# Interleaving the first two input units of a two-layer hybrid trunk, with the head of the kernel reordered

## Chip, core and metric

The kernel runs on one core of one Trainium2 chip. The metric is the device time of one execution in microseconds (us). Time before: 1334.67 us, the median of three runs (1334.59 to 1341.18).

## The reference, cut to what matters

Input x is 512 positions by 1024 features, and there are two layers of this form (layer 0 and layer 1):

```python
for l in range(2):
    h = rms_norm(x, norm_mix_g[l])
    aq, ak, av, rq, rk, rv, rg, sz, sxbc, sdt = split(h @ w_in[l])
    ya = swa_sink_attention(aq, ak, av, ...)     # head group A
    yr = retention(rq, rk, rv, rg, ...)          # head group B
    ys = ssd_mixer(sz, sxbc, sdt, ...)           # head group C: conv with 4 taps, then SSD
    x = x + concat([ya, yr, ys]) @ w_out[l]
    h = rms_norm(x, norm_ffn_g[l])
    x = x + conv_ffn(h, ...)
return rms_norm(x, final_norm_g)
```

`rms_norm(x, g)` is x / sqrt(mean(x*x) + eps) * g. The mean runs over the 1024 features.

## The kernel before, in words

Features lie on partitions: x is 8 tiles (o = 0 to 7) of 128 features by 512 positions. All dense products are split into high and low parts: a weight w is w_hi + w_lo and an activation h is h_hi + h_lo, each part in the type fp32r, and a product is three matmuls (h_hi by w_hi, h_lo by w_hi, h_hi by w_lo).

**Units.** A dense unit Dn makes 128 output columns. Of a layer, D0 to D27 are the input projection, each over 8 tiles of k, 24 matmuls of 128x512. The output projection and the FFN follow. Unit n accumulates in the PSUM bank dense[n % 2], so it waits until VectorE has evacuated unit n - 2 (semaphore evac). All matmuls go through the helpers at line 924. In a unit (`unit`) the high parts of a pack's tiles come first (two matmuls for each k) and then the low parts of its weights.

**Weights.** They come as a stream of packs, 4 tiles of 128x128 in 256 KB each, into 4 slots. For each pack SyncE's queue issues the fetch into w_raw, ScalarE makes w_hi by a copy (lines 405 and 418), GpSimd makes w_lo by a subtraction (line 359). `unit_tiles` and `segments` (SEGS, UNIT_END, PACK_END) lay the units into packs; `weight_stream` on the host fills the packs in the same order. ScalarE splits ahead: at step D of unit n it goes up to two packs behind the unit's last pack, or four where it has something to await there. The fetch of pack 4 in layer 0 is issued behind the eight transfers of the attention bias (lines 301 to 307).

**The norm.** The gain g is in h, and 1/sqrt of the mean (rstd) is multiplied in when a unit is evacuated. So D0 can start before rstd is known, but no unit of the input projection can be evacuated. For each tile o, ScalarE makes h_hi (line 381) and the square (386), VectorE makes h_lo (607) and adds the square to ssq (613), all in `norm_tile`. Square o waits for the addition o - 2, since there are two square buffers. In layer 0 this runs while x is being fetched (lines 291 to 295); for the later norms it runs behind the evacuations of the units before. The step NORM on TensorE (`norm`) is one matmul of ones by ssq into bank mix5. In `rms` ScalarE turns it into rstd: Ln (391) and Exp (394), each with a table load of its own. DT is the projection onto the eight dt columns, 24 matmuls into the same bank mix5; it waits until Ln has read the bank.

**The order.** SCHEDULE is a list written by hand, which every engine follows in program order. It begins `D0 NORM D1 DT D2 DTB D3 D4 DTC D5 D6 DTD D7 D8 TOK`. VectorE evacuates each D with rstd (line 664). D0, D1, D3, D4, D6 and D7 hold conv columns (U_CONV): behind each of these evacuations VectorE runs four dependent tap instructions (671 and 674), and ScalarE a silu (446). D2, D5 and D8 are evacuated only. VectorE's parts of DT, DTB, DTC and DTD (687 to 708) are a chain of small instructions on 8 partitions, with ScalarE's parts (467 to 475) between them. VectorE enters each layer by waiting for rstd; behind this wait stand two memsets (627, 628) and wdt_lo (630), and then the steps.

**The start.** TensorE first waits for `rel` and makes two small matmuls for the attention bias, and then goes to D0.

Of the kernel before, what the change touches and what calls it, by code (L numbers as in the profile page):

```python
# [19 lines left out]
D, S, P = 1024, 512, 128  # L20
# [11 lines left out]
SLOTS = 4  # L32
# [17 lines left out]


def segments():


    units, unit_end, pack_end, at, n = [], [], {}, 0, 0
    for tiles in unit_tiles():
        runs, k = [], 0
        while k < tiles:
            m = min(4 - at % 4, tiles - k)
            n += 1  # L60
            runs.append((at // 4, at % 4, k, m))
            at, k = at + m, k + m
            pack_end[(at - 1) // 4] = n
        units.append(runs)
        unit_end.append(n)
    return units, unit_end, [pack_end[i] for i in range(at // 4)], n
# [7 lines left out]
SCHEDULE = (  # L74
# [92 lines left out]
def build(nc, a, out):  # L167
    f32, f32r = mybir.dt.float32, mybir.dt.float32r
    ALU, ACT, AX = mybir.AluOpType, mybir.ActivationFunctionType, mybir.AxisListType
    with ExitStack() as ctx:  # L170
# [100 lines left out]
        f_scaled, f_conv, f_silu = sem("f_scaled"), sem("f_conv"), sem("f_silu")  # L271
        f_prod, f_hi, f_lo = sem("f_prod"), sem("f_hi"), sem("f_lo")
        relt_mm, relt_ready, rel_written = sem("relt_mm"), sem("relt_ready"), sem("rel_written")
        bias_loaded, setup_done = sem("bias_loaded"), sem("setup_done")
# [13 lines left out]
        def _(sp):  # L288
            sp.dma_start(p_all[:, :], a["params"]).then_inc(p_loaded, 16)
            sp.dma_start(ar("relh")[0:32, :], a["rel"]).then_inc(rel_loaded, 16)  # L290
            for o in range(KD):
                sp.dma_start(x[:, o, :], a["xT"][o]).then_inc(x_loaded[o], 16)
                if o % 2:
                    s = o // 2
                    sp.dma_start(w_raw[:, s, :], a["w"][s]).then_inc(raw_loaded[s], 16)
# [68 lines left out]
        def _(act):  # L364
# [10 lines left out]
            def norm_tile(e, o, l_evac):  # L375

                if l_evac is None:
                    act.wait_ge(x_loaded[o], 16)
                else:
                    act.wait_ge(evac, l_evac)  # L380
                nc.scalar.activation(h_hi[:, o, :], x[:, o, :], ACT.Copy,  # L381
                                     scale=gcol(e, o)).then_inc(h_hi_ready, 1)
                if o >= 3:
# [15 lines left out]
            act.wait_ge(p_loaded, 16)  # L399
            first_packs = {2: (0,), 5: (1,), KD - 1: (2, 3)}  # L400
            for o in range(KD):
                norm_tile(0, o, None)
                for s in first_packs.get(o, ()):
                    act.wait_ge(raw_loaded[s], 16)
                    nc.scalar.activation(w_hi[:, s, :], w_raw[:, s, :], ACT.Copy).then_inc(hi_ready, 1)  # L405
            act.wait_ge(c_loaded, 16 * N_CONST_LOADS)

# [173 lines left out]
        def _(dve):  # L581
# [10 lines left out]
            def gcol(e, o):  # L592
                return par["g"][:, bass.ds(e * KD + o, 1)]

            for i in range(6):
                V.memset(rstd[:, i:i + 1], 0.0).then_inc(m_free[i], 1)
# [7 lines left out]
            def norm_tile(e, o):  # L604

                dve.wait_ge(h_hi_ready, e * 8 + o + 1)
                V.scalar_tensor_tensor(h_lo[:, o, :], x[:, o, :], gcol(e, o), h_hi[:, o, :].bitcast(f32),  # L607
                                       ALU.mult, ALU.subtract).then_inc(h_lo_ready, 1)
                if o:
                    dve.wait_ge(sq_ready, e * 8 + o + 1)  # L610
                    if o > 1:
                        dve.wait_ge(ssq_added, e * 7 + o - 1)
                    V.tensor_tensor(ssq[:, :], ssq[:, :], sq[:, o % 2, :], ALU.add).then_inc(ssq_added, 1)  # L613

            for o in range(KD):
                norm_tile(0, o)
            dve.wait_ge(c_loaded, 16 * N_CONST_LOADS)
            with dve.Fori(0, DEPTH) as l:
                base[0] = l * DVE_LINKS
                links[0] = 2  # L620
                dve.wait_ge(rstd_ready, l * 2 + 1)

                def lo_from(dst, src, hi, done):
# [6 lines left out]
                V.tensor_tensor(wdt_lo[:, :], wdt_raw[:, bass.ds(l * 64, 64)], wdt_hi[:, :].bitcast(f32),  # L630
                                ALU.subtract).then_inc(wdt_lo_ready, 1)
                for name in SCHEDULE:
                    step, n = step_of(name)
# [286 lines left out]
        def _(pe):  # L920
            T = nc.tensor

            def mm(dst, lhsT, rhs, start=True, stop=True):
                return T.matmul(dst, lhsT, rhs, start=start, stop=stop)  # L924

            pe.wait_ge(rel_loaded, 16)

            mm(dense[0][0:8, 0:191], relw, relh).then_inc(relt_mm, 1)
            mm(dense[1][0:8, 0:8], relw, relw).then_inc(run_done, SEG0)
            pe.wait_ge(relt_ready, 1)  # L930

            def unit(bankno, number, runs, src_hi, src_lo, wait_for_tile=None):

                pe.wait_ge(evac, number + 1)
                d = dense[bankno][:, :]
                last = runs[-1][3] + runs[-1][4] - 1
# [38 lines left out]
            with pe.Fori(0, DEPTH) as l:  # L975
                def dense_unit(n, src, wait_for_tile=None):
                    runs = [(p % SLOTS, l * N_PACKS + p, t0, k0, m) for p, t0, k0, m in SEGS[n]]
                    unit(n % 2, l * N_UNITS + n, runs, *src, wait_for_tile)

                def ret_tile(k):  # L980
# [278 lines left out]
def weight_stream(w_in, w_out, w_up, w_down):  # L1259
# [14 lines left out]

    def unit(w, out_cols):
        tiles.extend(w[P * k:P * k + P][:, out_cols] for k in range(w.shape[0] // P))

    for l in range(DEPTH):
        for c in cols:
            unit(w_in[l], c)  # L1280
        for part in range(3):
# [64 lines left out]
```

## Time and profile before

| | us |
|---|---|
| median of three runs | 1334.67 |
| the runs | 1334.59, 1334.67, 1341.18 |
| the profiled execution: time | 1339.34 |
| its span | 1337.6 |
| TensorE busy | 1296.2 (97%) |
| weight load on TensorE | 1042.3 (78%) |
| VectorE busy | 634.7 (47%) |
| ScalarE busy | 627.4 (47%) |
| GpSimd busy | 577.7 (43%) |

The span is what the profile covers; the execution's own time has a little more around it. Busy shares are averages over the whole span, and stages differ. PE is TensorE, PEld its weight load, DVE VectorE, ACT ScalarE, POOL GpSimd and SP SyncE with its DMA queue. PEclk is the granted TensorE clock as a share of 2.4 GHz. At the head, until the first change that it recorded, the profile shows 1.00 whatever the pace; there the durations of the matmuls tell it.

### The profile page before, as it was taken

Reading aid. Unit: us, or ns where it says so; the run is one execution under the profiler, and the core shown is the slowest. Engines: PE = TensorE matmul, PEld = TensorE weight load, DVE = VectorE, ACT = ScalarE, POOL = GpSimd, SP = SyncE. Lnnn points to the kernel's source line nnn. Section 1 sums busy time; section 2 is a strip of 40 time slices with the busy share of each in tenths; the row PEclk is TensorE's granted clock in tenths of the full one; section 3 lists DMA queues with packets and bytes.
Section 4 is the critical chain, followed back from the end, with each engine's and each line's share of the span. In section 5 each row is a group of like instructions: output and inputs, shape, how many; then the busy total and the mean of one; then the engine's idle time right before and its main releaser. Section 6 shows DMA issues by size and latency. Waiting matters only on the chain.

```text
span 1337.6 us, 21561 instructions
## 1 busy us (share of the span) xinstructions
PE 1296.2 (97%) x6130; PEld 1042.3 (78%) x6130; DVE 634.7 (47%) x957; ACT 627.4 (47%) x961; POOL 577.7 (43%) x433
## 2 busy tenths in 40 slices
PE   6999999999999999999999999999999999999995
PEld 4777777777888888888877777777788888888884
DVE  6845567366444203443267546664744430144423
ACT  6432285356666323333363225825676652233433
POOL 2533344154444544444444334333454444444443
PEclk9999999999999999999999999999999999999998
DMA  6334222132333322332223432121323333223232
GB/s 193 111 104 111 64 79 76 35 103 79 102 94 94 110 95 84 97 99 95 98 81 104 118 87 79 58 69 55 103 88 101 100 97 101 95 94 94 94 103 102
DMA packets 77305, 125.32 MB, mean 94 GB/s; under 512 B 7672, under 2 KB 20248, under 8 KB 77112
## 3 DMA queue, kind: packets, MB, share of 16 engines
q1 hardware_dynamic: 77240, 124.47, 30.2%
q8 instruction: 38, 0.62, 0.2%
q14 instruction: 27, 0.22, 0.0%
HBM read 121.89 MB, written 2.55 MB: 93 GB/s over the span
## 4 chain that ended last, share of the span: by engine, by line
PE 81%; DVE 10%; issue 5%; ACT 2%; DVEq 1%; DMA 0%; ACTq 0%; SPq 0%
PE dense L924 74%; PE mix L924 6%; DVE arena L674 2%; DVE h_lo L607 2%; DVE ssq L613 1%; ACT w_hi L418 1%; PE mix L1095 1%; DVE arena L696 1%; DVE arena L769 0%; DVE arena L671 0%; DVE pad L664 0%; DMA x<-in_xT 0%; DVE mx L799 0%; DVE arena L805 0%; DVE arena L872 0%
## 5 line engine op out<-in xcount | busy, mean ns | idle before, releaser
L359 POOL TENSOR_TENSOR w_lo<-w_raw,w_hi 128x512 fp32r<-128x512 f32 x428 | 577.3, 1365 | 749.7 <-ACT w_hi L418 735.0
L924 PE MATMUL dense<-h_hi,w_hi 128*128 128x512 f32 x1152 | 458.1, 398 | 14.8 <-ACT w_hi L405 6.3
L924 PE MATMUL dense<-h_lo,w_hi 128*128 128x512 f32 x1152 | 450.8, 391 | 0.0
L418 ACT ACTIVATE w_hi<-w_raw 128x512 fp32r<-128x512 f32 x424 | 249.3, 622 | 186.1 <-PE dense L924 181.3
L924 PE MATMUL dense<-h_hi,w_lo 128*128 128x512 f32 x1152 | 309.8, 391 | 0.0
L924 PEld LDWEIGHTS dense<-h_hi,w_hi 128*128 128x128 f32 x1152 | 217.7, 189 | 67.7 <-issue 14.1
L924 PEld LDWEIGHTS dense<-h_lo,w_hi 128*128 128x128 f32 x1152 | 217.6, 189 | 46.7 <-issue 2.5
L924 PEld LDWEIGHTS dense<-h_hi,w_lo 128*128 128x128 f32 x1152 | 217.4, 189 | 45.7
L924 PE MATMUL dense<-m_hi,w_hi 128*128 128x512 f32 x544 | 217.3, 400 | 3.2 <-ACT w_hi L418 2.5
L924 PE MATMUL dense<-m_lo,w_hi 128*128 128x512 f32 x544 | 211.9, 390 | 0.0
L924 PE MATMUL dense<-m_hi,w_lo 128*128 128x512 f32 x544 | 146.8, 389 | 0.0
L924 PEld LDWEIGHTS dense<-m_hi,w_hi 128*128 128x128 f32 x544 | 102.1, 188 | 29.0 <-DVE x L655 3.3
L924 PEld LDWEIGHTS dense<-m_lo,w_hi 128*128 128x128 f32 x544 | 102.1, 188 | 23.0 <-issue 2.4
L924 PEld LDWEIGHTS dense<-m_hi,w_lo 128*128 128x128 f32 x544 | 102.1, 188 | 21.4
L908 DVE TENSOR_TENSOR x<-dense,x 128x512 f32<-128x512 f32 x32 | 22.1, 691 | 193.7 <-PE dense L924 193.7
L889 DVE SCALAR_TENSOR_TENSOR arena<-arena,params 128x512 f32<-128x512 f32 x44 | 53.1, 1206 | 62.7 <-ACT arena L559 62.7
L886 DVE TENSOR_TENSOR arena<-dense,rstd 128x512 f32<-128x512 f32 x44 | 30.5, 692 | 107.1 <-PE dense L924 107.1
L566 ACT ACTIVATE m_hi<-arena 128x512 f32 x44 | 27.8, 632 | 92.5 <-DVE arena L899 92.5
L381 ACT ACTIVATE h_hi<-x,params 128x512 fp32r<-128x512 f32 x40 | 28.9, 722 | 74.4 <-DVE x L908 67.8
L564 ACT ACTIVATE arena<-arena 128x512 f32<-128x512 f32 x44 | 27.8, 632 | 72.1 <-DVE arena L893 72.1
L924 PE MATMUL mix<-arena 64*128 64x128 f32 (+4 forms) x696 | 60.3, 299 | 1.1 <-DVE arena L769 1.1
L924 PEld LDWEIGHTS mix<-arena 128*64 128x64 f32 (+3 forms) x696 | 45.0, 160 | 15.8 <-issue 8.6
(160 smaller groups left out, 990.8 us busy)
## 6 DMA issues: line engine op xcount, KB each, us to landing
w_raw<-in_w SPq DMA_DIRECT2D x428, 256.0 KB, 2.6
arena<-cum_rows SPq DMA_DIRECT2D x8, 512.0 KB, 6.3
x<-in_xT SPq DMA_DIRECT2D x8, 256.0 KB, 5.5
out_y<-arena SPq DMA_DIRECT2D x8, 256.0 KB, 2.2
arena<-exp_rows SPq DMA_DIRECT2D x12, 128.0 KB, 7.0
consts<-in_consts SPq DMA_DIRECT2D x1, 1283.0 KB
rel_scratch<-arena SPq DMA_DIRECT2D x1, 382.0 KB
bias<-rel_scratch SPq DMA_DIRECT2D x8, 32.0 KB, 2.0
```

Source lines behind the costliest of these rows:

```text
L359: nc.gpsimd.tensor_tensor(w_lo[:, s, :], w_raw[:, s, :], w_hi[:, s, :].bitcast(f32), ALU.subtract).then_inc(lo_ready, 1)
L381: nc.scalar.activation(h_hi[:, o, :], x[:, o, :], ACT.Copy, scale=gcol(e, o)).then_inc(h_hi_ready, 1)
L418: nc.scalar.activation(w_hi[:, slot, :], w_raw[:, slot, :], ACT.Copy).then_inc(hi_ready, 1)
L564: nc.scalar.activation(fs, fy, ACT.Silu).then_inc(f_silu, 1)
L566: nc.scalar.activation(m_hi[:, bass.ds(i, 1), :], fg.unsqueeze(1), ACT.Copy)\
L607: V.scalar_tensor_tensor(h_lo[:, o, :], x[:, o, :], gcol(e, o), h_hi[:, o, :].bitcast(f32), ALU.mult, ALU.subtract).then_inc(h_lo_ready, 1)
L613: V.tensor_tensor(ssq[:, :], ssq[:, :], sq[:, o % 2, :], ALU.add).then_inc(ssq_added, 1)
L674: ins = V.scalar_tensor_tensor(dst, pad[:, n % 2, k:k + S], taps[:, bass.ds(l * 30 + t * 5 + k, 1)], dst, ALU.mult, ALU.add)
L886: V.tensor_tensor(fpad[:, 2:2 + S], dense[0][:, :], rstd[:, :], ALU.mult).then_inc(evac, 1)
L889: ins = V.scalar_tensor_tensor(fy, fpad[:, 1:1 + S], par["fconv"][:, bass.ds(fi * 4 + 1, 1)], fy, ALU.mult, ALU.add)
L908: V.tensor_tensor(x[:, o, :], dense[n % 2][:, :], x[:, o, :], ALU.add).then_inc(evac, 1)
L924: return T.matmul(dst, lhsT, rhs, start=start, stop=stop)
```

## The change

1. D0 and D1 are interleaved by four k tiles in every layer: D0 with k 0 to 3, D1 with k 0 to 3, D0 with k 4 to 7, D1 with k 4 to 7, in two banks. A new function `stream` gives this order to `segments` and `weight_stream`. On TensorE all of D0 and the first half of D1 are in the step D0.
2. SCHEDULE begins `D0 D1 NORM DT` in place of `D0 NORM D1 DT`, in both layers.
3. In layer 0 the weight packs are fetched and split behind x tiles 0, 3, 5 and 7, where before they were fetched behind tiles 1, 3, 5 and 7 and split behind 2, 5, 7 and 7.
4. In layer 0 ScalarE makes all high parts (and the four packs between them) first and then all squares; VectorE makes all low parts and then all additions.
5. VectorE's memsets and wdt_lo stand ahead of its wait for rstd, in both layers.
6. TensorE multiplies zeros in fp32 (from `lg`, cleared first by VectorE): one matmul ahead of the wait for `rel`, two behind the small ones. They go to the bank dense[1], whose first real matmul clears it.

```diff
+def stream():
+    pieces = [(0, 0, 4), (1, 0, 4), (0, 4, 4), (1, 4, 4)]
+    return pieces + [(u, 0, tiles) for u, tiles in enumerate(unit_tiles()) if u > 1]
...
-    "D0 NORM D1 DT D2 DTB D3 D4 DTC D5 D6 DTD D7 D8 TOK D9 SA0 D10 D11 SB0 SA1 D12 D13 SB1 SA2 D14 D15 "
+    "D0 D1 NORM DT D2 DTB D3 D4 DTC D5 D6 DTD D7 D8 TOK D9 SA0 D10 D11 SB0 SA1 D12 D13 SB1 SA2 D14 D15 "
...
+            first_packs = {0: (0,), 3: (1,), 5: (2,), KD - 1: (3,)}
             for o in range(KD):
                 sp.dma_start(x[:, o, :], a["xT"][o]).then_inc(x_loaded[o], 16)
-                if o % 2:
-                    s = o // 2
+                for s in first_packs.get(o, ()):
                     sp.dma_start(w_raw[:, s, :], a["w"][s]).then_inc(raw_loaded[s], 16)
...
-            first_packs = {2: (0,), 5: (1,), KD - 1: (2, 3)}
+            first_packs = {0: (0,), 3: (1,), 5: (2,), KD - 1: (3,)}
             for o in range(KD):
-                norm_tile(0, o, None)
+                act.wait_ge(x_loaded[o], 16)
+                nc.scalar.activation(h_hi[:, o, :], x[:, o, :], ACT.Copy,
+                                     scale=gcol(0, o)).then_inc(h_hi_ready, 1)
                 for s in first_packs.get(o, ()):
                     act.wait_ge(raw_loaded[s], 16)
                     nc.scalar.activation(w_hi[:, s, :], w_raw[:, s, :], ACT.Copy).then_inc(hi_ready, 1)
+            for o in range(KD):
+                square(0, o)
...
+            V.memset(lg[:, 0:S], 0.0).then_inc(warm_ready, 1)
...
             for o in range(KD):
-                norm_tile(0, o)
+                low(0, o)
+            for o in range(1, KD):
+                add_square(0, o)
...
-                dve.wait_ge(rstd_ready, l * 2 + 1)
...
                 V.tensor_tensor(wdt_lo[:, :], wdt_raw[:, bass.ds(l * 64, 64)], wdt_hi[:, :].bitcast(f32),
                                 ALU.subtract).then_inc(wdt_lo_ready, 1)
+                dve.wait_ge(rstd_ready, l * 2 + 1)
...
+            pe.wait_ge(warm_ready, 1)
+            mm(dense[1][:, :], lg[:, 0:P], lg[:, 0:S])
             pe.wait_ge(rel_loaded, 16)
 
             mm(dense[0][0:8, 0:191], relw, relh).then_inc(relt_mm, 1)
             mm(dense[1][0:8, 0:8], relw, relw).then_inc(run_done, SEG0)
+            mm(dense[1][:, :], lg[:, 0:P], lg[:, 0:S])
+            mm(dense[1][:, :], lg[:, 0:P], lg[:, 0:S])
             pe.wait_ge(relt_ready, 1)
...
-                        if n < N_IN:
-                            dense_unit(n, h_src, h_tile(l * 2) if n == 0 else None)
+                        if n == 0:
+                            pe.wait_ge(evac, l * N_UNITS + 1)
+                            paired_seg(0, 0, h_tile(l * 2))
+                            pe.wait_ge(evac, l * N_UNITS + 2)
+                            paired_seg(1, 0)
+                            paired_seg(0, 1, h_tile(l * 2))
+                        elif n == 1:
+                            paired_seg(1, 1)
+                        elif n < N_IN:
+                            dense_unit(n, h_src)
```

`paired_seg(n, i)` does segment i of unit n by `segs`, the inner part of `unit` without its wait for the bank. `square`, `low` and `add_square` are the parts of `norm_tile`.

## Rows read from the trace of the kernel before

**Rows 1.** The page: the span, and the engines' shares of the chain that ended last.
```profile
span 1337.6 us, 21561 instructions
...
PE 81%; DVE 10%; issue 5%; ACT 2%; DVEq 1%; DMA 0%; ACTq 0%; SPq 0%
```

**Rows 2.** Chain of waits, longest pieces in time order: start us, us, what.
```profile
64.13 12.72 PE dense L924 x48
...
327.43 343.07 PE dense L924 x1512
...
717.45 11.19 PE dense L924 x48
```

**Rows 3.** Windows: A:B length, busy us (instructions) by engine, PEclk, DMA share, GB/s.
```profile
679.85:717.40 37.55, 35.50 (x157) 26.59 (x155) 31.75 (x36) 17.38 (x27) 19.41 (x14) 1.00 0.26 85
26.05:64.10 38.05, 35.54 (x157) 26.63 (x155) 32.21 (x36) 17.47 (x26) 19.40 (x14) 1.00 0.35 115
```

**Rows 4.** Waits of PE: 26 to 64.2 us first, then 682 to 718 us.
```profile
PE dense L924 <- DVE arena L664: 2.5, 1, 2.5
...
PE dense L924 <- DVE arena L664: 2.1, 1, 2.1
```

**Rows 5.** Timeline, second layer's head: start us, us, engine line operation [idle before].
```profile
670.57 0.47 PE L924 MATMUL dense<-h_hi,w_hi 128*128 128x512 f32 x1
...
676.14 1.02 PE L924 MATMUL mix<-ssq,consts 128*128 128x512 f32 x2
...
679.22 0.63 ACT L394 ACTIVATE rstd<-rstd 128x512 f32<-128x512 f32 x1
...
680.26 0.68 DVE L664 TENSOR_TENSOR pad<-dense,rstd 128x512 f32<-128x512 f32 x1
...
682.46 0.39 PE L924 MATMUL mix<-h_hi,wdt_hi 128*8 128x512 f32 x1
```

**Rows 6.** The page: DMA issues of x, KB each, median us to landing.
```profile
x<-in_xT SPq DMA_DIRECT2D x8, 256.0 KB, 5.5
```

**Rows 7.** Timeline, first layer's head.
```profile
6.13 0.91 SPq L292 DMA_DIRECT2D x<-in_xT  x2
...
9.66 0.69 DVE L613 TENSOR_TENSOR ssq<-ssq,sq 128x512 f32<-128x512 f32 x1
...
17.24 1.28 ACT L430 ACT_TABLE_LOAD   x1
...
18.54 0.26 ACT L430 ACTIVATE wdt_hi<-wdt_raw 128x64 fp32r x1
18.81 1.28 ACT L391 ACT_TABLE_LOAD   x1
19.06 1.76 DVE L613 TENSOR_TENSOR ssq<-ssq,sq 128x512 f32<-128x512 f32 x1
...
21.68 1.70 PE L924 MATMUL mix<-ssq,consts 128*128 128x512 f32 x2
...
25.42 0.63 ACT L394 ACTIVATE rstd<-rstd 128x512 f32<-128x512 f32 x1
...
26.47 0.68 DVE L664 TENSOR_TENSOR pad<-dense,rstd 128x512 f32<-128x512 f32 x1
```

**Rows 8.** Timeline, weights of the first layer's second block: issue and first use.
```profile
27.70 19.39 SPq L315 DMA_DIRECT2D w_raw<-in_w  x10
...
30.52 1.33 ACT L418 ACTIVATE w_hi<-w_raw 128x512 fp32r<-128x512 f32 x2 [4.47 <-DMA w_raw<-in_w]
```

**Rows 9.** Timeline, one TensorE matmul of the first unit before and after its pace changed.
```profile
11.67 0.63 PE L924 MATMUL dense<-h_lo,w_hi 128*128 128x512 f32 x1
...
16.53 0.40 PE L924 MATMUL dense<-h_lo,w_hi 128*128 128x512 f32 x1
```

**Rows 10.** Windows of 1 us around the two restarts of TensorE.
```profile
64.00:65.00 1.00, 0.87 (x2) 0.78 (x3) 0.80 (x3) 0.00 (x0) 0.38 (x1) 0.50 0.77 203
...
717.00:718.00 1.00, 0.55 (x2) 0.49 (x3) 0.99 (x2) 0.00 (x0) 0.71 (x1) 1.00 0.50 186
```

More of the change, by code:

```diff
@@ L49, in unit_tiles @@
     return [8] * N_IN + [4] * 24 + [8] * 24 + [12] * 8 + [8] * 20 + [10] * 8
+def stream():
+    pieces = [(0, 0, 4), (1, 0, 4), (0, 4, 4), (1, 4, 4)]
+    return pieces + [(u, 0, tiles) for u, tiles in enumerate(unit_tiles()) if u > 1]
 def segments():
[L55 to L59, printed above, removed]
+    units, unit_end, pack_end, at, n = [[] for _ in unit_tiles()], [0] * len(unit_tiles()), {}, 0, 0
+    for u, k, tiles in stream():
+        end = k + tiles
+        while k < end:
+            m = min(4 - at % 4, end - k)
             n += 1
-            runs.append((at // 4, at % 4, k, m))
+            units[u].append((at // 4, at % 4, k, m))
             at, k = at + m, k + m
             pack_end[(at - 1) // 4] = n
-        units.append(runs)
-        unit_end.append(n)
+        unit_end[u] = n
     return units, unit_end, [pack_end[i] for i in range(at // 4)], n
@@ L272, in build @@
         f_prod, f_hi, f_lo = sem("f_prod"), sem("f_hi"), sem("f_lo")
+        warm_ready = sem("warm_ready")
         relt_mm, relt_ready, rel_written = sem("relt_mm"), sem("relt_ready"), sem("rel_written")
@@ L375, in norm_tile, with square @@
             def norm_tile(e, o, l_evac):
[L377 to L380, printed above, removed]
+                act.wait_ge(evac, l_evac)
                 nc.scalar.activation(h_hi[:, o, :], x[:, o, :], ACT.Copy,
                                      scale=gcol(e, o)).then_inc(h_hi_ready, 1)
+                square(e, o)
+            def square(e, o):
                 if o >= 3:
@@ L604, in norm_tile, with low @@
             def norm_tile(e, o):
+                low(e, o)
+                if o:
+                    add_square(e, o)
+            def low(e, o):
                 dve.wait_ge(h_hi_ready, e * 8 + o + 1)
@@ L608, in norm_tile, with add_square @@
                                        ALU.mult, ALU.subtract).then_inc(h_lo_ready, 1)
[L609 to L613, printed above, removed]
+            def add_square(e, o):
+                dve.wait_ge(sq_ready, e * 8 + o + 1)
+                if o > 1:
+                    dve.wait_ge(ssq_added, e * 7 + o - 1)
+                V.tensor_tensor(ssq[:, :], ssq[:, :], sq[:, o % 2, :], ALU.add).then_inc(ssq_added, 1)
             for o in range(KD):
-                norm_tile(0, o)
+                low(0, o)
+            for o in range(1, KD):
+                add_square(0, o)
             dve.wait_ge(c_loaded, 16 * N_CONST_LOADS)
@@ L934, in unit, with segs @@
                 pe.wait_ge(evac, number + 1)
+                last = runs[-1][3] + runs[-1][4] - 1
+                segs(bankno, runs, last, src_hi, src_lo, wait_for_tile)
+            def segs(bankno, runs, last, src_hi, src_lo, wait_for_tile=None):
                 d = dense[bankno][:, :]
-                last = runs[-1][3] + runs[-1][4] - 1
                 for slot, pack, t0, k0, m in runs:
@@ L978, in dense_unit, with paired_seg @@
                     unit(n % 2, l * N_UNITS + n, runs, *src, wait_for_tile)
+                def paired_seg(n, i, wait_for_tile=None):
+                    p, t0, k0, m = SEGS[n][i]
+                    segs(n, [(p % SLOTS, l * N_PACKS + p, t0, k0, m)], KD - 1, *h_src, wait_for_tile)
                 def ret_tile(k):
@@ L1273, in weight_stream, with unit @@
     tiles = []
-    def unit(w, out_cols):
-        tiles.extend(w[P * k:P * k + P][:, out_cols] for k in range(w.shape[0] // P))
+    def unit(w, out_cols, k0=0, m=None):
+        end = w.shape[0] // P if m is None else k0 + m
+        tiles.extend(w[P * k:P * k + P][:, out_cols] for k in range(k0, end))
     for l in range(DEPTH):
-        for c in cols:
-            unit(w_in[l], c)
+        for u, k0, m in stream()[:N_IN + 2]:
+            unit(w_in[l], cols[u], k0, m)
         for part in range(3):
```

## The prediction, made before the change was run

> **What bounds the kernel now.** Start with the page: the chain that ended last is TensorE for 81% of 1337.6 us [rows 1], so wherever TensorE is fed, only work taken off it helps, and the change takes none off. What it can move are the places where TensorE waits. The chain in order of time shows two, one a layer: TensorE restarts with unit D7 at 64.13 in layer 0 and at 717.45 in layer 1 [rows 2]. The list of its waits says for what: 2.5 and 2.1 us for line 664, the evacuation of D5, which frees the bank that D7 accumulates in [rows 4].
>
> VectorE is late there for a reason that lies far ahead. Nothing can be evacuated before rstd exists. The windows from the end of rstd to the D7 restart are 38.05 us in layer 0 and 37.55 us in layer 1, with VectorE busy 32.21 and 31.75 of them, and most of the rest goes into hand-offs between dependent instructions [rows 3]. Evacuation, four-tap convolution, evacuation, convolution, and the dt arithmetic follow one another in program order. So **in both layers D7 starts some 38 us after rstd, whatever TensorE does in between, as long as it stays ahead**. The question for the change is when rstd comes in each layer. Behind D7, TensorE sets the end again (343.07 us without a break in layer 0 [rows 2]), so a shift of D7 reaches the end in full.
>
> **Layer 1, the loop body as every layer has it.** Before, the first unit takes 676.14 - 670.57 = 5.57 us, then NORM's matmul runs, and D1 and DT follow [rows 5]. The change puts D1's 24 matmuls ahead of NORM. A matmul costs 343.07 / 1512 = 0.227 us [rows 2], so NORM, Ln and Exp move back by 24 x 0.227 = **5.45 us**. Nothing arrives late here that the interleaving could hide: the h tiles are there when D0 runs, and TensorE does not wait. The two memsets and wdt_lo now run ahead of the wait for rstd; Exp ends at 679.22 + 0.63 = 679.85 and the first evacuation starts at 680.26, 0.41 later [rows 5], of which about 0.08 should stay, a gain of 0.33. Line 664 starts 5.45 - 0.33 = **5.1 us later**, at 685.4.
>
> NORM and DT use the same bank. Before, D1 hid the time in which ScalarE read it. Now DT waits for Ln, which ended a table load (1.28 us [rows 7]) before Exp, at 677.94, and will end at 683.4; DT began at 682.46 [rows 5], so TensorE is 1.0 us later through D2 to D6. That costs nothing more: D6 ended at 717.45 - 2.1 = 715.35, will end at 716.35, and D7 waits until 717.45 + 5.1 = 722.55. The wait grows from 2.1 to 6.2 us. ScalarE now splits three packs instead of two behind Exp, ahead of the first silu; D1's step has one fewer, and TensorE needs them only after DT: zero.
>
> The longer wait has a price of its own, the clock. After layer 0's 2.5 us wait the granted clock was 0.50, its lower level of 1.2 GHz; after layer 1's 2.1 us it stayed at 1.00 [rows 4, 10]. The same 48 matmuls then took 12.72 against 11.19 us [rows 2], 1.53 us. A 6.2 us wait should drop it: **+1.5 us**. Bounds: 0, if it does not fall, and 2.7 us, from the head of the kernel, where matmuls held 0.63 us from 11.67 or earlier and reached 0.40 by 16.53 [rows 9], a slow stretch of over 5 us at about half speed. I take 1.5, since it is the same place of the program. The Trainium skill (TensorE: Matmul & The Clock Gate, Part 1) says that half speed is the default state and activity releases it; layer 0's wait agrees, layer 1's shows that an idle stretch of 2.1 us need not trip it. This rule speaks for the zeros in the head and against the wait that grows here.
>
> **Layer 0, the head.** Here x is still loading. ScalarE's order changes from high part and square by turns to all high parts with the packs, then all squares. The last x is issued at about 6.6 and lands some 5.5 us later, perhaps 12.6, since the fetches overlap [rows 6, 7]; a weight moved ahead of or behind it shifts this by one 256 KB transfer at most. Before, ScalarE reached it late; now high part 7 ends near 13.4, and the last pack near 14.0. VectorE's low parts, with one tensor more to read than an addition of 0.69 us [rows 7] and longer beside GpSimd (the addition at 19.06 took 1.76), keep up but for a backlog of about one: low part 7 ends near 15.3.
>
> TensorE needs the low parts and 48 matmuls. I put the first tile with its pack at 7.3 and tile 3 at 10.7, by ScalarE's pace of some 0.6 us for each tile or pack and the spacing of the fetches. Some 40 matmuls then remain, 9.1 us at full pace: D1 ends at 19.8. The zeros (one matmul of 1.7 us at the slow pace [rows 7] ahead of rel, two behind it, on a waiting engine) end about 7.3, when the first tile and pack are ready, so they cost nothing; with no cover they would cost up to 1.7 us.
>
> But the sum of squares comes later in the order. Square 3 waits for the first addition, and that stands behind low part 7 on VectorE. First addition until 16.0, then six at 0.69 + 0.05 [rows 7]: the last ends at 20.4, against 19.06 + 1.76 = 20.82 before. The last square starts at the end of addition 5, 19.0, and ends 19.6. Behind it ScalarE has, as before, a table load, wdt_hi and a second load: 1.28 + 0.26 + 1.28 [rows 7], so Ln cannot begin before 22.5, and this is what ends last. NORM, ready at 20.4, needs 0.95 to 1.7 us and is hidden. Before, NORM began at 21.68 and took 1.70, so Ln began near 23.4 and Exp ended at 26.05, 2.65 later [rows 7]. Exp now ends at 25.15, and line 664, without the 0.42 us of memsets and wdt_lo, starts near 25.2 instead of 26.47: **1.2 us earlier**. D7 starts near 62.9. Bounds: 2.2 us earlier if only NORM binds, 1.4 us later if TensorE falls back to the slow pace while it waits for tiles (see the rivals).
>
> The Trainium skill (ScalarE: Activation LUTs, on table sets) says that copy is in every set, so that a load is needed only when the function wants another one. The trace has a load directly ahead of wdt_hi's copy, which follows other copies at line 405. By the page that load would not be there and the gain would be 2.2 us; the row decides.
>
> TensorE's time won here is not used. The second block of weights is issued at 27.70, behind the bias transfers, and first split at 30.52 [rows 8]; D2 cannot start before 31.1, ends D6 at 31.1 + 5 x 5.45 = 58.4, and waits 4.5 us for D7, slow behind it as before.
>
> **The sum.** 5.1 + 1.5 - 1.2 = **+5.4 us**. The profiled execution took 1339.34 us (span 1337.6), 4.7 above the median of 1334.67 of the runs shown, one of which is at 1341.18. I set the difference on the median: **1340.1 us**, 0.4% slower. About 0.5%, 6.7 us, is what can be told from no change, so this lands inside it, close to its upper edge.
>
> **Rivals.**
> (a) The clock costs more. In layer 0 the tiles come about every 0.7 us while a tile's two matmuls take 0.45 us at full pace, so the zeros may raise the clock only for it to fall while TensorE is half idle; then D1 ends near 22.5 to 24 and the 1.2 us are gone or turned into a loss of 1.4. In layer 1 the slow stretch may last 5 us or more. For it: 2.5 us of idling sufficed once [rows 4, 10]. The price is 5.1 + 2.7 + 0 to 1.4 = +7.8 to +9.2, 1342.5 to 1343.9. It decides as soon as these two cost 1.3 us more than my values, which carries the total over 6.7. Slower; chance 0.33.
> (b) The chain on VectorE is not rigid: part of the 38 us was waiting for TensorE, and with TensorE earlier in layer 0 it shrinks. VectorE did wait for D2, but ScalarE's dt steps ran meanwhile. If all of TensorE's lead of some 5 us counted in layer 0, and only the 1.0 us of DT in layer 1, the result would be -4, 1330.7. Against it: both layers have the same 38 us though their starts differ. 0.07; with a faster VectorE beside it, 0.05 for a gain beyond 0.5%.
> (c) The zeros do not raise the clock: D0 starts at the slow pace as before, D1 ends near 22.5, Exp near 26.2. Layer 0 then gains 0.3 and the result is +6.3, 1341.0. 0.15.
> (d) Ln is free earlier, layer 0 gains 2.2: +4.4, 1339.1. 0.1.
> My own case keeps 0.35. Runs differ by several us, which widens all of them.
>
> **The numbers.** 1335.5 to 1345.5 takes in (a), (c), (d) and the low end 5.1 + 0 - 2.2 = +2.9, with a few us for the spread of runs; (b) stays outside. Slower by over 0.5%: (a) and the upper part of (c) with the spread, less what (a) leaves inside, 0.35; faster 0.05; the same 0.60.
>
> **What would show it.** Right: in layer 1 Ln about 5.4 us later behind D0's start, TensorE waiting about 6 us for line 664 ahead of D7 with the granted clock at 0.50 behind it, and the window from rstd to D7 still about 38 us. In layer 0, rstd about 1 us earlier with ScalarE's table loads directly ahead of Ln, and D2 waiting for the pack of line 418. Wrong: that window shortens when TensorE is earlier, line 664 starts less than 4 us later in layer 1, or D1 of layer 0 ends behind 22 us.

## The result, and the profile after

The changed kernel takes 1346.32 us (median of 7 runs, 1344.63 to 1347.71), the kernel before 1336.63 us (median of 7, 1334.59 to 1341.18): a ratio of **1.0062, 95% interval 1.0046 to 1.0077**, some 8 us more (the two medians alone are 9.7 apart). The profiled executions are 8.3 us apart in span, so the two traces can be read against each other mark by mark. First the page of the changed kernel and its chain of waits in order of time (start us, us, what), the lines that answer to [rows 1, 2]:

```profile
span 1345.9 us, 21576 instructions
...
PE 81%; DVE 11%; issue 4%; ACT 3%; DVEq 0%; ACTq 0%; DMA 0%; SPq 0%
```

```profile
63.84 13.72 PE dense L947 x48
...
327.88 354.08 PE dense L947 x1560
...
723.67 12.79 PE dense L947 x48
...
986.75 343.06 PE dense L947 x1512
```

D7 of layer 0 starts at 63.84, 0.3 earlier than before; D7 of layer 1 at 723.67, 6.2 later. The 48 matmuls behind each take 13.72 and 12.79 us, where before it was 12.72 and 11.19. By 986.75, the start of the last long stretch, 7.4 us are lost.

The windows from the end of Exp to the start of D7, which answer to [rows 3] (the columns are the same; layer 1 first):

```profile
685.50:723.67 38.17, 32.90 (x138) 24.89 (x136) 31.88 (x33) 17.24 (x26) 19.34 (x14) 0.96 0.26 84
26.06:63.84 37.78, 31.61 (x137) 23.68 (x135) 31.39 (x33) 17.48 (x27) 19.19 (x14) 0.98 0.38 114
```

38.17 and 37.78 us: the distance is kept, although TensorE was busy for 32.90 and 31.61 us of them and not 35.5. Its waits, in layer 0 (up to 64.2 us) and then in layer 1 (660 to 740 us), which answer to [rows 4]:

```profile
PE dense L947 <- DVE arena L687: 3.4, 1, 3.4
PE dense L947 <- ACT w_hi L430: 2.8, 2, 2.5
```

```profile
PE dense L947 <- ACT w_hi L430: 3.5, 1, 3.5
PE dense L947 <- DVE arena L687: 1.8, 1, 1.8
```

Now the head of layer 1 in the timeline, which answers to [rows 5]:

```profile
670.80 0.47 PE L947 MATMUL dense<-h_hi,w_hi 128*128 128x512 f32 x1
...
681.81 1.02 PE L947 MATMUL mix<-ssq,consts 128*128 128x512 f32 x2
...
683.61 0.39 PE L947 MATMUL mix<-h_hi,wdt_hi 128*8 128x512 f32 x1 [0.78 <-ACT rstd L399]
...
684.87 0.63 ACT L402 ACTIVATE rstd<-rstd 128x512 f32<-128x512 f32 x1
...
685.63 0.69 DVE L687 TENSOR_TENSOR pad<-dense,rstd 128x512 f32<-128x512 f32 x1 [8.85 <-ACT rstd L402]
...
691.90 0.68 DVE L687 TENSOR_TENSOR pad<-dense,rstd 128x512 f32<-128x512 f32 x1
```

From D0's first matmul to the start of NORM there are 11.01 us where there were 5.57; Exp ends at 684.87 + 0.63 = 685.50, 14.70 us behind D0's start, where it was 9.28. That is **+5.4 us**. DT waits 0.8 us for Ln, until 683.61. And the head of layer 0, which answers to [rows 7]:

```profile
1.46 6.52 PE L947 MATMUL dense<-arena 128*128 128x512 f32 x10 [1.46 <-DVE arena L607]
...
8.05 0.39 PE L947 MATMUL dense<-h_lo,w_hi 128*128 128x512 f32 x1
...
16.02 5.46 DVE L634 TENSOR_TENSOR ssq<-ssq,sq 128x512 f32<-128x512 f32 x7
...
19.92 0.63 ACT L394 ACTIVATE sq<-x 128x512 f32<-128x512 f32 x1 [0.16 <-DVE ssq L634]
...
20.57 1.28 ACT L442 ACT_TABLE_LOAD   x1
...
21.61 0.30 PEld L947 LDWEIGHTS mix<-ssq,consts 128*128 128x128 f32 x2 [0.84 <-issue]
...
23.43 0.69 ACT L399 ACTIVATE rstd<-mix,params 128x512 f32<-128x512 f32 x1
...
26.19 0.69 DVE L687 TENSOR_TENSOR pad<-dense,rstd 128x512 f32<-128x512 f32 x1 [3.69 <-ACT rstd L402]
```

The zeros hold TensorE from 1.46, matmuls run at the full pace at 8.05 (0.39 us), and NORM begins at 21.61. But Ln starts at 23.43, behind ScalarE's second table load, and Exp ends at 26.06, where it ended at 26.05 before. Last, the clock, in windows of 2 us of the changed kernel (columns as in [rows 10]):

```profile
704.00:706.00 2.00, 2.00 (x7) 1.53 (x6) 1.88 (x2) 1.98 (x4) 2.00 (x2) 0.53 0.00 0
...
724.00:726.00 2.00, 2.00 (x7) 1.55 (x6) 1.51 (x3) 0.00 (x0) 0.00 (x0) 0.66 0.61 214
...
64.00:66.00 2.00, 2.00 (x5) 1.61 (x6) 1.65 (x3) 0.00 (x0) 0.11 (x1) 0.50 0.74 226
```

Its mean was 0.53 behind the wait for the pack in layer 1, 0.66 behind that for D7, since a part of this window ran at full pace, and 0.50 behind D7's start in layer 0.

**The account of the 8.3 us.** Up to D0 of layer 1, +0.2 (670.80 against 670.57): D7 0.3 earlier, its 48 matmuls 1.0 slower, 0.5 less in the rest of the layer. Exp behind D0's start, +5.4. D7 behind Exp in layer 1, +0.6 (38.17 against 717.45 - 679.85 = 37.60). The clock behind D7, +1.6. Up to the last long stretch, -0.4. At the end +0.9: the last NORM took 2.04 us, as this timeline row of the changed kernel shows, against 1.10 before (at 1325.72). Both stand behind a wait of 3.35 us, but the granted clock was 0.55 in the window 1332 to 1334 here and 0.99 in 1324 to 1327 before:

```profile
1333.16 2.04 PE L947 MATMUL mix<-ssq,consts 128*128 128x512 f32 x2 [3.35 <-issue]
```

### The profile page after: what moved, and what is told of

It reads as the page before. It is cut to its first block, busy times and chain, and to the rows that moved or that the text cites. A ratio compares the mean times of both kernels' runs of the same rounds, so it can differ in the third digit from the quotient of the medians.

```text
span 1345.9 us, 21576 instructions
## 1 busy us (share of the span) xinstructions
PE 1303.7 (97%) x6136; PEld 1043.9 (78%) x6136; DVE 636.9 (47%) x958; ACT 627.9 (47%) x961; POOL 575.9 (43%) x433
## 4 chain that ended last, share of the span: by engine, by line
PE 81%; DVE 11%; issue 4%; ACT 3%; DVEq 0%; ACTq 0%; DMA 0%; SPq 0%
PE dense L947 73%; PE mix L947 6%; DVE h_lo L626 2%; DVE arena L697 2%; DVE arena L893 1%; DVE ssq L634 1%; ACT w_hi L430 1%; DVE arena L694 1%; DVE arena L895 1%; PE mix L1139 1%; DVE arena L792 1%; DVE arena L719 0%; DVE pad L687 0%; DVE arena L938 0%; DVE x L678 0%
## 5 line engine op out<-in xcount | busy, mean ns | idle before, releaser
L385 ACT ACTIVATE h_hi<-x,params 128x512 fp32r<-128x512 f32 x32 | 23.2, 725 | 74.3 <-DVE x L931 67.8
```

Source lines behind the costliest of these rows:

```text
L385: nc.scalar.activation(h_hi[:, o, :], x[:, o, :], ACT.Copy, scale=gcol(e, o)).then_inc(h_hi_ready, 1)
```

## The experiments

Twelve kernels ran. The times of the kernel before drift by a few us from one group of runs to the next, so each ratio is to the runs of the kernel before that were made beside it, and where a step of a few tenths is at stake the trace decides, not the time.

### NORM back between D0 and D1

```diff
-    "D0 D1 NORM DT D2 DTB ...
+    "D0 NORM D1 DT D2 DTB ...
```

> The changed kernel with NORM back between D0 and D1 in the order (D0 still interleaved with D1, so NORM now stands behind 36 matmuls instead of 48). Theory (rstd sets D7 through VectorE's chain): in layer 1 NORM comes 12 x 0.227 = 2.7 us earlier, and so do Exp, line 687 and the start of D7; D1's second half covers Ln, so TensorE no longer waits 0.8 us ahead of DT. In layer 0 ScalarE's table load ahead of Ln (ends 23.4) binds and rstd stays at 26.06. Total 2.7 us under the changed kernel, about 1343.6. Rival (TensorE's own order sets the end, the place of NORM does not matter): at most the two waits ahead of DT, and D7 of layer 1 stays at its time.

Measured: 1347.5 us, ratio 1.0061 (1.0038 to 1.0084), no faster than the changed kernel, where 2.7 us less was expected. Its Exp in the timeline and its chain of waits:

```profile
682.17 0.63 ACT L402 ACTIVATE rstd<-rstd 128x512 f32<-128x512 f32 x1
```

```profile
721.00 13.93 PE dense L947 x48
737.84 6.91 PE dense L947 x24
```

Exp ends at 682.80, 2.70 earlier than 685.50, and D7 starts at 721.00, 2.67 earlier than 723.67. The chain theory is met to 0.03 us. But the 48 matmuls then took 13.93 instead of 12.79, and the next 24, D9 behind TOK, 6.91 instead of 5.57: 2.5 us went to the clock in this execution (granted 0.50 in 722 to 726 and in 738 to 740). In layer 0, Exp ended at 26.50 and not at 26.06, and D7 came at 64.86, 1.0 later than in the changed kernel. So rstd sets D7, and what it brings can be lost right behind it.

### The order alone, on the kernel before

```diff
-    "D0 NORM D1 DT D2 DTB ...
+    "D0 D1 NORM DT D2 DTB ...
```

> The kernel before with one edit: NORM behind D1 in the order, nothing else. Theory: in layer 1 rstd, and D7 with it, come 5.45 us later; in layer 0 as well, since D1's matmuls now lie ahead of NORM, 5.2 us; the wait ahead of D7 in layer 1 grows beyond 2.5 us and its 48 matmuls take 12.7 instead of 11.2. Total +10 to +13 us on the kernel before, 1347 to 1350. Rival (only the wait of DT for Ln counts): +1 to +2 us.

Measured: 1350.75 us, ratio 1.0084 (1.006 to 1.0108), about 11 us slower, as expected. That is more than the 8 us of the whole change; the two intervals overlap, but in the traces too D7 of layer 1 is later here, 725.89 against 723.67. The chain:

```profile
67.29 12.81 PE dense L924 x48
...
725.89 12.83 PE dense L924 x48
```

In layer 1 Exp ends at 687.70 + 0.63 = 688.33 and D7 starts 37.56 us later; in layer 0 Exp ends at 28.91 + 0.63 = 29.54, 3.5 later than before, and D7 starts at 67.29, 3.2 later, where 5.2 was expected. In the changed kernel the new head gives these 3.5 us of layer 0 back. Layer 1 has nothing of the kind.

### The wait ahead of D7 filled

```diff
+                        if n == 7:
+                            pe.wait_ge(m_free[2], ready("AT0", 0, l))
+                            for _ in range(2):
+                                mm(M[2][:, :], ones[:, :], consts["cos"][:, :])
```

> The changed kernel with two fp32 matmuls of 128x512 (0.9 us each, into a bank that is free there) on TensorE directly ahead of its wait for D7's bank, in both layers. They fill 1.8 us of waits of 3.4 and 1.8 us. Theory (the clock falls in the wait and D7 and D8 pay for it): granted clock 1.00 behind D7's start in layer 1, its 48 matmuls 11.2 instead of 12.8 us; in layer 0 perhaps the same, 11.2 instead of 13.7. Total 1.6 to 4.1 us under the changed kernel. Rival (the slow stretch is on no path): no change, or up to 0.1 us more. If the wait still drops the clock the run is no test of the price.

Measured: 1345.8 us, ratio 1.0051 (1.0034 to 1.0068). The chain, and a window of layer 1:

```profile
64.30 11.19 PE dense L947 x48
78.16 7.20 PE dense L947 x24
...
723.18 11.15 PE dense L947 x48
737.01 7.18 PE dense L947 x24
```

```profile
738.00:740.00 2.00, 2.00 (x7) 1.57 (x6) 0.00 (x0) 1.22 (x3) 1.20 (x1) 0.54 0.58 166
```

The price of the clock at this place is shown: with the wait filled the granted clock is 1.00 behind D7's start (windows 64 to 66 and 723 to 727), and the 48 matmuls take 11.19 and 11.15 us instead of 13.72 and 12.79. But D9, behind the small matmuls of TOK, now takes 7.20 and 7.18 us, and the window there stands at 0.54. Most of the gain is given back one stage later, and the total is the changed kernel's within the intervals, not the 1.6 to 4.1 us less that was expected.

### Without the zeros

```diff
-            V.memset(lg[:, 0:S], 0.0).then_inc(warm_ready, 1)
...
-            pe.wait_ge(warm_ready, 1)
-            mm(dense[1][:, :], lg[:, 0:P], lg[:, 0:S])
...
-            mm(dense[1][:, :], lg[:, 0:P], lg[:, 0:S])
-            mm(dense[1][:, :], lg[:, 0:P], lg[:, 0:S])
```

> The changed kernel without the three zero matmuls, their memset and its semaphore. Theory (ScalarE's squares and table loads set rstd in layer 0, and TensorE has slack there): TensorE starts D0 slow and ends D1 later than at 21.0, but NORM has to be done only by 23.4, so rstd comes at 26.1 to 27 and the total is within 1 us of the changed kernel. Rival (the zeros carry a gain of the clock that counts): D1 ends near 23 or later and rstd comes 1.5 us or more later, and the total rises by that.

Measured: 1347.08 us, ratio 1.0061 (1.0038 to 1.0083). TensorE in the timeline:

```profile
12.19 0.63 PE L946 MATMUL dense<-h_lo,w_hi 128*128 128x512 f32 x1
...
13.62 0.39 PE L946 MATMUL dense<-h_hi,w_hi 128*128 128x512 f32 x1
...
21.81 1.02 PE L946 MATMUL mix<-ssq,consts 128*128 128x512 f32 x2
```

The first matmuls take 0.63 us, the last of them at 12.19, and the full pace comes by 13.62. D1's last four matmuls start at 20.90 instead of 20.13, and still NORM begins at 21.81, only 0.2 later than with the zeros, since there it waits for the last addition; Ln starts at 23.53 against 23.43, behind ScalarE's table load in both. **The zeros raise the clock and bring nothing**: they work where TensorE has slack. In this execution D7 even starts earlier than in the changed kernel, at 63.27 in layer 0 and at 721.58 in layer 1, and it loses this behind TOK, where 24 matmuls take 8.40 us instead of 5.57 at a granted clock of 0.50:

```profile
737.30 8.40 PE dense L946 x24
```

### High parts and squares by turns

```diff
                 nc.scalar.activation(h_hi[:, o, :], x[:, o, :], ACT.Copy,
                                      scale=gcol(0, o)).then_inc(h_hi_ready, 1)
+                square(0, o)
...
-            for o in range(KD):
-                square(0, o)
...
-            for o in range(KD):
-                low(0, o)
-            for o in range(1, KD):
-                add_square(0, o)
+            for o in range(KD):
+                norm_tile(0, o)
```

> The changed kernel with only the head's order of high parts, squares, low parts and additions put back by turns, as before. Theory (all high parts first gets the low parts and so D1 out early, and that is what lets NORM stand behind D1 in layer 0; the squares behind them are free up to ScalarE's table loads): the additions end near 20.8 instead of 21.5, but low part 7 and pack 3 come at 17 to 19 instead of 16.1, D1 ends near 23.2 instead of 21.0, NORM behind it, and rstd comes near 26.9 instead of 26.06. D7 of layer 0 some 0.8 us later, layer 1 as in the changed kernel. Rival (the squares are what holds rstd back, and the order by turns is better here too): rstd at 24.6 to 25.5, D7 0.6 to 1.4 us earlier.

Measured: 1347.3 us, ratio 1.0054 (1.0034 to 1.0074). ScalarE in the timeline:

```profile
24.95 0.69 ACT L399 ACTIVATE rstd<-mix,params 128x512 f32<-128x512 f32 x1 [3.28 <-PE mix L944]
```

Ln now waits 3.28 us for NORM, since D1 ends late, and Exp ends at 26.95 + 0.63 = 27.58, 1.5 later than in the changed kernel. D7 of layer 0 starts at 65.47, 1.6 later. The direction is the theory's, the size twice the expected 0.8. So with NORM behind D1 the new order of the head is worth 1.5 us of rstd. With NORM between D0 and D1 (the first experiment) the new order had Exp end at 26.50, against 26.05 in the kernel before: no gain is seen there.

### Two packs at D0's step, and the memsets back

The first kernel leaves one pack to D1's step; the second has, besides, VectorE's wait back ahead of the memsets and wdt_lo.

```diff
-                            hi_to(SEGS[n][-1][0] + SLOTS)
+                            hi_to(SEGS[n][-1][0] + SLOTS - (n == 0))
```

> The changed kernel with ScalarE splitting two packs instead of three in the step D0 (the third goes to D1's step). Theory (GpSimd's third low part lies beside VectorE's first convolution and stretches it by 0.85 us, which I had counted as nothing): in layer 1 the second evacuation of line 687 comes 5.4 us after the first, as before the change, not 6.3, and D7 0.6 to 0.9 us earlier. Rival (the same GpSimd work lands on the second convolution instead): D7 at the same distance of 38.2 us from the end of Exp, no gain. By time below what can be told; the trace decides.

```diff
                 links[0] = 2
+                dve.wait_ge(rstd_ready, l * 2 + 1)
...
-                dve.wait_ge(rstd_ready, l * 2 + 1)
                 for name in SCHEDULE:
```

> The version of the changed kernel with two packs split at D0's step, with the two memsets and wdt_lo put back behind VectorE's wait for rstd. Theory (the chain behind rstd grew from 37.55 to 38.15 us because VectorE now begins 0.3 us earlier against GpSimd and D1's first tap meets the next low part, 1.66 instead of 0.55 us): in layer 1 D1's first tap back at 0.55 us and D7 again 37.5 to 37.6 us behind Exp's end, so that moving the memsets ahead of the wait had no gain there. Rival (the longer chain comes from another part of the change, the interleaving or the order of the packs): D7 at 38.1 us or more behind Exp's end, the 0.3 us of the memsets on top.

VectorE of layer 1 in the timeline, first with two packs and then with the memsets back as well:

```profile
690.35 0.69 DVE L687 TENSOR_TENSOR pad<-dense,rstd 128x512 f32<-128x512 f32 x1
691.62 1.66 DVE L694 TENSOR_SCALAR arena<-pad,params 128x512 f32<-128x512 f32 x1 [0.58 <-DVE pad L687]
```

```profile
689.06 0.68 DVE L687 TENSOR_TENSOR pad<-dense,rstd 128x512 f32<-128x512 f32 x1
689.95 0.55 DVE L694 TENSOR_SCALAR arena<-pad,params 128x512 f32<-128x512 f32 x1 [0.21 <-DVE pad L687]
```

With two packs the second evacuation comes 5.47 us behind the first (684.88), as before the change, but D1's first tap (line 694) now takes 1.66 us, and D7 starts at 722.90, 38.15 behind Exp's end at 684.75. My theory of the third pack fell, and the rival's result held: the same GpSimd work lands on the next convolution. With the memsets back, that tap takes 0.55 us, and D7 starts here, in the chain of waits:

```profile
721.02 12.77 PE dense L947 x48
```

721.02 - (682.86 + 0.63) = 37.53 us, the distance of the kernel before. The numbers are the theory's, but its reason, the 0.3 us by which VectorE starts earlier, does not stand. In layer 1 this lead is gone with D0's first tap, which ends 2.18 us behind Exp both before (681.23 + 0.80) and after (686.60 + 1.08), and with two packs the second evacuation stands at 5.60 us behind Exp as it did before. What differs is the pause ahead of D1's first tap, the number in brackets: 0.58 us here, 0.21 before. And the version without the zeros, whose memsets stand ahead of the wait and which splits three packs, has the short pause and a distance of 721.58 - 684.06 = 37.52 us:

```profile
691.35 0.55 DVE L693 TENSOR_SCALAR arena<-pad,params 128x512 f32<-128x512 f32 x1 [0.21 <-DVE pad L686]
```

The pause goes with the kernel: 0.21 us in both layers of the kernel before, of its version with the order alone, of the one without zeros and of the one with the memsets back; 0.63 us in layer 0 and 0.58 in layer 1 of all the others, the changed kernel in both its profiles included. **So in layer 1 part 5's gain of 0.3 us never reaches D7, and the 0.6 us come with a longer pause, behind which D1's first tap stands beside a low part of GpSimd. What makes the pause longer stays open.** (The version with two packs: 1346.56 us, ratio 1.0048, 1.0029 to 1.0067. The last ran once, 1344.09 us, which tells nothing by itself. The memsets back with three packs was not run.)

### NORM early in layer 1

```diff
                             paired_seg(1, 0)
+                            with pe.If(l > 0):
+                                norm(l * 2, "NORM", l)
                             paired_seg(0, 1, h_tile(l * 2))
...
                     elif step == "NORM":
-                        norm(l * 2, name, l)
+                        with pe.If(l < 1):
+                            norm(l * 2, name, l)
```

> The changed kernel with NORM of layer 1 alone (a branch on the layer) behind D1's first half, 24 matmuls after D0's start, as many as before the change; layer 0 keeps it behind D1. Theory: rstd of layer 1 5.4 us earlier, D7 5.4 us earlier (at 718.2 to 718.5 by the changed kernel's clock), which gives back the change's main loss; total 5.4 us less, 1341, if the slow stretches of the clock are the same, 1339.5 to 1343.5 with one more or one less. Rival (the clock's slow stretches make most of the difference and the place of NORM little): total above 1344.

Measured: 1341.17 us, ratio **1.0012 (0.9993 to 1.0031)**: the change's loss is gone. Timeline of layer 1's head, and chain:

```profile
670.21 0.47 PE L947 MATMUL dense<-h_hi,w_hi 128*128 128x512 f32 x1
...
675.78 1.02 PE L947 MATMUL mix<-ssq,consts 128*128 128x512 f32 x2
...
678.88 0.63 ACT L402 ACTIVATE rstd<-rstd 128x512 f32<-128x512 f32 x1
```

```profile
717.69 11.19 PE dense L947 x48
```

Exp ends 9.30 us behind D0's start, as before the change (9.28), D7 starts at 717.69, and the 48 matmuls behind it take 11.19 us, the full pace. This one edit was repeated beside the changed kernel:

> The changed kernel once more, unaltered, on the same chip and in the same rounds as the next one. Expected 7 to 9 us above the kernel before, with rstd, D7 and the wait for the pack at the same places, and the number and place of slow stretches of the clock perhaps not: they are what I take the runs' spread of several us for.

> The version with NORM early in layer 1 alone, once more beside the changed kernel. Theory (NORM's place in layer 1 carries 5.4 us and one slow stretch): 5 to 8 us under the changed kernel of the same rounds. Rival: under 4 us, the rest of the difference seen before being the chip's.

Measured: the changed kernel 1346.88 us, ratio 1.0058 (1.0038 to 1.0078); with NORM early in layer 1, 1340.99 us, ratio 1.0021 (1.0004 to 1.0039). 5.9 us between them, in the range of the theory. In the changed kernel's second profile D7 of layer 0 starts at 64.95 and its 48 matmuls take 12.76 us, and those of layer 1 11.18; the unit that waited for its pack took 8.63 instead, from 703.98 on, and VectorE then waited 1.2 us for it, so that D7 came 38.80 us behind Exp and not 38.17. The same kernel has its slow matmuls at other places from one execution to the next. The spread of the runs goes with the clock too: of the 25 runs of the kernel before that were made here, the fastest, 1335.02 us, had a mean granted clock of 0.996, and the slowest, 1342.87 us, one of 0.991.

### Two versions meant to be faster

The first has D0 and D1 one after the other, NORM behind D0 in layer 0 and behind its first half in layer 1, wdt_hi behind Exp, and the wait ahead of D7 filled in layer 0.

```diff
-    pieces = [(0, 0, 4), (1, 0, 4), (0, 4, 4), (1, 4, 4)]
-    return pieces + [(u, 0, tiles) for u, tiles in enumerate(unit_tiles()) if u > 1]
+    return [(u, 0, tiles) for u, tiles in enumerate(unit_tiles())]
...
-    "D0 D1 NORM DT D2 DTB ...
+    "D0 NORM D1 DT D2 DTB ...
...
                             paired_seg(0, 0, h_tile(l * 2))
-                            pe.wait_ge(evac, l * N_UNITS + 2)
-                            paired_seg(1, 0)
+                            with pe.If(l > 0):
+                                norm(l * 2, "NORM", l)
                             paired_seg(0, 1, h_tile(l * 2))
-                        elif n == 1:
-                            paired_seg(1, 1)
...
                     elif step == "NORM":
-                        norm(l * 2, name, l)
+                        with pe.If(l < 1):
+                            norm(l * 2, name, l)
...
+                rms(0, "NORM", l)
                 nc.scalar.activation(wdt_hi[:, :], wdt_raw[:, bass.ds(l * 64, 64)], ACT.Copy)\
                     .then_inc(wdt_hi_ready, 1)
-                rms(0, "NORM", l)
...
                             V.tensor_tensor(dst, d[:, :], rstd[:, :], ALU.mult).then_inc(evac, 1)
+                        if n == 0:
+                            dve.wait_ge(wdt_hi_ready, l + 1)
+                            V.tensor_tensor(wdt_lo[:, :], wdt_raw[:, bass.ds(l * 64, 64)],
+                                            wdt_hi[:, :].bitcast(f32), ALU.subtract).then_inc(wdt_lo_ready, 1)
...
+                        if n == 7:
+                            with pe.If(l < 1):
+                                for _ in range(2):
+                                    mm(M[2][:, :], ones[:, :], consts["cos"][:, :])
```

> A version meant to beat both. D0 and D1 one after the other; the head's order and the zeros of the changed kernel; NORM behind D0 in layer 0, and in layer 1 already behind D0's first half; wdt_hi and wdt_lo made behind Exp and behind the first evacuation, so that one of ScalarE's two table loads ahead of Ln goes; two filling matmuls ahead of D7's wait in layer 0. Theory (rstd sets D7): rstd at 25.3 in layer 0 and D7 near 63.1; in layer 1 rstd 1.6 to 2 us earlier after D0's start than before the change, TensorE no longer waits ahead of D7 (at 715 to 716). Total 3 to 5 us under the kernel before. Rival (slow stretches appear elsewhere, as behind TOK with the filled wait): between 1 us less and 1 us more than before.

Measured: 1340.19 us, ratio 1.0001 (0.9984 to 1.0018). Chain, and VectorE of layer 1:

```profile
325.89 343.03 PE dense L947 x1512
...
716.22 11.21 PE dense L947 x48
730.33 6.82 PE dense L947 x24
```

```profile
692.61 0.69 DVE L683 TENSOR_TENSOR arena<-dense,rstd 128x512 f32<-128x512 f32 x1 [3.08 <-PE dense L947]
```

Layer 0 gains 1.5 us up to its long stretch (325.89 against 327.43), but not by rstd: Exp ends 0.6 us earlier, D7 starts at 64.43, 0.3 later than before and not near 63.1, and its 48 matmuls, with the wait filled, take 11.15 us instead of 12.72. In layer 1 Exp ends 3.2 us earlier than before (676.70), but D7 starts only 1.2 earlier: VectorE now waits 3.08 us for TensorE to finish D2. Here the chain is no longer VectorE's alone. D9 at 730.33 took 6.82 us, 1.3 more than before, which takes the 1.2 back; the spans are 1337.4 us here and 1337.6 before.

The second is the version with NORM early in layer 1 with two packs at D0's step and wdt_hi and wdt_lo behind Exp, both edits as shown above:

> The kernel with NORM early in layer 1 (changed kernel otherwise), with two more edits: two packs instead of three split at D0's step, and wdt_hi and wdt_lo made behind Exp and behind the first evacuation. No filling. Theory: rstd of layer 0 at 25.3, D7 near 63.3; in layer 1 the second evacuation 5.4 us after the first, D7 0.6 us earlier after D0's start than in the version it comes from. About 1 to 2 us under the kernel before, and 7 us or more under the changed kernel on the same chip. Rival (the slow stretches of the clock outweigh it): within 1.5 us of the kernel before, either way.

Measured: 1339.94 us, ratio 1.0007 (0.9988 to 1.0025). Exp of layer 0 ends at 25.75 and D7 starts at 63.34, 0.8 earlier than before; D7 of layer 1 at 717.30. The spans say 0.6 us less than before (1337.0 against 1337.6), and the times cannot tell it. No version beat the kernel before by what a measurement can show.

## Why the prediction was right, and where it was wrong

The direction and the cause were right; the size was too small: 5.4 us forecast, 8.3 in the profiles and 8 by the ratio. The median of 1346.32 lies 0.8 above the range, and the slowdown of 0.62% (0.46 to 0.77) beyond the bound of 0.5%, which had 0.35 and not the larger chance. A part of this is the starting point: I set the forecast on a median of 1334.67 from three runs, and with all seven it is 1336.63.

- **D7 some 38 us behind rstd, whatever TensorE does.** Right: 37.78 and 38.17 us, and 37.5 to 38.4 in layer 1 of nine other profiles. It was 38.8 in two (the order by turns, and the changed kernel's second profile), where VectorE waited 1.1 and 1.2 us for TensorE, and 39.5 in the combined version: there the condition that TensorE stays ahead failed. Shown by moving NORM by 12 matmuls (D7 moved by 2.67) and by 24 (D7 back to its place, 5.9 us in the time).
- **Layer 1, rstd 5.45 us later.** Right: 5.42. DT waited 0.8, where I had 1.0.
- **Memsets ahead of the wait, 0.33 us gained.** Right at the start of the chain (line 687 starts 0.13 behind Exp, not 0.41, and 5.1 us later behind D0's start than before, as forecast), wrong at its end: in layer 1 the gain was gone after one tap, and D7 came 0.6 later behind Exp, a term that I did not have. Its cause is shown only as far as the longer pause ahead of D1's first tap. The pack that I costed at zero shifts the second evacuation by 0.8 us (6.27 behind the first, and 5.47 with two packs), but D7 by nothing: 38.17 and 38.15.
- **A wait of 6.2 us ahead of D7.** Only 1.8. TensorE had already waited 3.5 us for the pack of D4, which ScalarE splits behind the dt steps, and these follow rstd too. I had looked for the next late thing only at D7. The sum is the same, the place is not, and each of the two waits can pull the clock down.
- **The clock, +1.5 in layer 1.** Right in this profile: 12.79 - 11.19 = 1.60; in the kernel's second profile the slow matmuls stood at D4. Missing from the sum: layer 0's stretch, 1.0 longer than before, and the last NORM, 0.9. Rival (a) had the mechanism but put it in D0 and D1, where the clock stayed up from 8.05 on; its price of 7.8 to 9.2 us takes in what was measured, but by luck, since neither of its two terms (2.7 in layer 1, up to 1.4 in layer 0's D0 and D1) came true.
- **Layer 0, rstd 1.2 us earlier.** This is the step of the sum that failed most: 0.0. The bound was the right one, ScalarE's two table loads behind the last square, but that square ended at 20.55, not 19.6. The first addition began at 16.02, when I had it end, and the seven took 0.78 us each, hand-off included, not 0.74. The Trainium skill's statement (ScalarE: Activation LUTs, on table sets) that copy needs no load of its own was set against the row: the load at 20.57 ahead of wdt_hi was again there. With wdt_hi moved behind Exp no load stands ahead of its copy (25.36 and 25.66 in the two versions), as the page has it; one load instead of two stands ahead of Ln, which started at 22.82 and 23.12. So it is the place in the program that goes with the load, not the copy, and in this kernel one load has to be counted ahead of the first function of the loop body.
- **The sum.** From D0 to D7 in layer 1 it is 5.4 - 0.3 + 0.9 = 6.0 (forecast 5.1): rstd, the earlier start of line 687, and what the chain behind it lost. The clock took 1.6 + 1.0 + 0.9 = 3.5 (forecast 1.5). D7 of layer 0 came 0.3 earlier (forecast 1.2), and the rest of the two layers gave back 0.5 and 0.4, which no run explains: 6.0 + 3.5 - 0.3 - 0.9 = 8.3.

## What to carry to other kernels

An edit to a loop body is paid in every pass. Here interleaving and a later NORM were fitted to the first pass, where data is late, and cost 5.4 us in the pass where nothing was late; a branch on the layer gave it back. Ask of each moved step what it releases, not what it costs where it stands: 24 matmuls put ahead of NORM added no work to TensorE and still delayed everything, since a chain of 38 us on another engine hangs on NORM's result. And in work with waits of 2 to 4 us on TensorE, allow for each such place, in every estimate, the 1.3 to 3.1 us that a slow stretch cost here.

## What was new about the hardware

The clock's lower level followed waits of 1.8 and 3.5 us here, though it did not follow one of 2.1 us at the same place before the change, nor one of 2.7 us with NORM early in layer 1. Filling the wait moved it behind TOK's small matmuls, where the kernel before had none in its profile. Where 24 or 48 matmuls ran slow in part, the price was 1.3 to 3.1 us, and one kernel's profiles differ in which places pay it. Three fp32 matmuls of zeros, on an otherwise idle engine, brought full pace by 8.05 us; without them it came between 12.2 and 13.62. And one instruction of VectorE, D1's first tap, took 0.55 us in layer 1 where it stood 0.21 us behind the evacuation ahead of it, and 1.66 us beside a low part of GpSimd where it stood 0.58 us behind. This pause was the same in every profile of a kernel and differed between kernels whose edits lay elsewhere.
